# A block-fused transformer kernel: VectorE keeps the first half of each weight residue, GpSimd takes the second

## The reference

```python
# block 2 (second_block)
hid = silu(x @ w_gate) * (x @ w_up)
ffn = hid @ w_down
ple = sigmoid(x @ w_ple_gate) * (p @ w_ple)
x = layer_norm(ALPHA * x + ffn + ple, ln2_g, ln2_b)
# block 3 (conv_ffn)
u = h @ w_up
uc = conv_b + sum(shift(u, 2 - i) * conv_w[i] for i in range(3))
gate, val = split(uc, 2)
y = (silu(gate) * val) @ w_down
```

## Time and profile before

| what | value |
|---|---|
| median of 3 runs | 4415.32 us (4413.2 to 4418.15) |
| profiled execution | 4419.46 us, its span 4418.1 us |
| PE busy | 3849.8 us (87%) |
| VectorE busy | 2018.2 us (46%) |
| ScalarE busy | 1107.3 us (25%) |
| GpSimd busy | 80.8 us (2%) |
| mean granted TensorE clock | 0.917 of full |

### The profile page before, as it was taken

The page is one execution under the profiler, slowest core; times in us unless marked ns, Lnnn a source line. Parts: engine busy times, 40 slices in busy tenths (PEclk is TensorE's granted clock), DMA queues, the critical chain, the costliest instruction groups (busy, mean ns, idle before and its releaser), DMA issues. The chain is left out here.

```text
span 4418.1 us, 59550 instructions
## 1 busy us (share of the span) xinstructions
PE 3849.8 (87%) x24448; PEld 3504.7 (79%) x24448; DVE 2018.2 (46%) x2880; ACT 1107.3 (25%) x1261; POOL 80.8 (2%) x151
## 2 busy tenths in 40 slices
PE   6997889999998979446999999995998769999897
PEld 5885678888887867235999999994875669999897
DVE  1554134344445445553555544444121246766545
ACT  1001122222220000001444433332011034444333
POOL 0000010000000001000000000000000000000000
PEclk9998988888888989768999999997998889999998
DMA  4675211111115748213455554451332234444453
GB/s 192 262 300 185 86 44 52 59 50 40 40 40 206 307 181 339 95 48 105 154 190 189 189 179 177 178 182 69 143 129 90 86 114 171 180 162 179 161 192 143
DMA packets 90682, 650.42 MB, mean 147 GB/s; under 512 B 10065, under 2 KB 10577, under 8 KB 12370
## 3 DMA queue, kind: packets, MB, share of 16 engines
q1 hardware_dynamic: 74304, 540.05, 33.8%
q0 software_dynamic: 13824, 100.67, 5.7%
q10 hardware_dynamic: 2450, 8.16, 0.5%
HBM read 646.74 MB, written 2.10 MB: 147 GB/s over the span
## 5 line engine op out<-in xcount | busy, mean ns | idle before, releaser
L391 PE MATMUL ps<-work,ring 128*128 128x256 f32 x5920 | 1298.2, 382 | 40.4 <-DVE work L1576 10.9
L391 PEld LDWEIGHTS ps<-work,ring 128*128 128x128 f32 x5920 | 1132.0, 192 | 200.6 <-DVE work L1576 11.8
L1338 DVE TENSOR_TENSOR ring_parts<-ring,ring_hi 128x1024 fp32r<-128x1024 f32 x568 | 689.3, 1225 | 726.2 <-ACT ring_hi L920 725.7
L920 ACT ACTIVATE ring_hi<-ring 128x1024 fp32r<-128x1024 f32 x568 | 599.3, 1059 | 940.0 <-PE ps L416 939.9
L414 PE MATMUL ps<-x_hi,ring_hi 128*128 128x256 f32 x1664 | 465.6, 280 | 22.4 <-DVE x_lo L1674 22.4
L415 PE MATMUL ps<-x_lo,ring_hi 128*128 128x256 f32 x1664 | 462.2, 278 | 0.0
L416 PE MATMUL ps<-x_hi,ring_parts 128*128 128x256 f32 x1664 | 460.4, 277 | 0.0
L414 PE MATMUL ps<-h_hi,ring_hi 128*128 128x256 f32 x1408 | 399.6, 284 | 48.0 <-DVE ring_parts L1338 26.2
L414 PE MATMUL ps<-hid_hi,ring_hi 128*128 128x256 f32 x1392 | 394.3, 283 | 37.3 <-DVE gu L1700 19.3
L415 PE MATMUL ps<-h_lo,ring_hi 128*128 128x256 f32 x1408 | 395.5, 281 | 0.0
L416 PE MATMUL ps<-h_hi,ring_parts 128*128 128x256 f32 x1408 | 394.7, 280 | 0.0
(11 more groups left out here) (371 smaller groups left out, 3935.6 us busy)
## 6 DMA issues: line engine op xcount, KB each, us to landing
ring<-in_weights SPq DMA_DIRECT2D x511, 1024.0 KB, 4.8
work<-in_ada POOLq DMA_DIRECT2D x96, 1024.0 KB, 8.1
resid<-in_lora ACTq DMA_DIRECT2D x9, 256.0 KB, 2.6
resid<-in_x SPq DMA_DIRECT2D x1, 2048.0 KB, 13.4
resid<-in_x ACTq DMA_DIRECT2D x1, 2048.0 KB, 8.8
out<-work SPq DMA_DIRECT2D x4, 512.0 KB, 2.6
con<-in_const ACTq DMA_DIRECT2D x1, 1666.0 KB, 13.6
con<-in_const ACTq DMA_DIRECT2D x1, 1028.0 KB
```

What stands on the lines that cost most here:

```text
L391: ins = mm(PS[:, b + m // 2, (m % 2) * T:(m % 2 + 1) * T], ws[:, k, m * P:(m + 1) * P], rhs(kc), start=(kc == 0 and m % 2 == 0), stop=(kc ...
L920: A(HI[:, 2 * (e % 2) + half, :], ring[:, n % RING, half * (SLOT // 2):(half + 1) * (SLOT // 2)], ACT.Copy)\
L1338: tt(lo, x, HI[:, e % 4, :].bitcast(F32), ALU.subtract).then_inc(S("lo_ready"), 1)
```

## The change

A slot's two residues get an engine each. VectorE subtracts the first half of each slot and counts in `lo_even`. GpSimd subtracts the second half and counts in `lo_odd`, in two loops of four slots a trip: 38 trips over `ffn2` and `down2`, which stand behind `fetch_modulations(1)`, and 33 trips over `ffn3` and `down3`, which stand behind the zeroing of `UP3`. TensorE waits for `lo_even` before a first half and for `lo_odd` before a second. Operands, shapes and ScalarE's part are as they were.

```diff
@@ by_parts (TensorE)
                 for half in range(2):
-                    v = 2 * e + half + 1
-                    pe.wait_ge(S("lo_ready"), v if i is None else v + i * 2 * step)
+                    pe.wait_ge(S("lo_even" if half == 0 else "lo_odd"), e + 1 if i is None else e + 1 + i * step)
@@ GpSimd
         fetch_modulations(1)
+        def split_odd(first, slots):
+
+            with gp.Fori(0, slots // RING) as i:
+                for n in range(first, first + RING):
+                    e = 2 * SPLIT_AT[n] + 1
+                    gp.wait_ge(S("hi_ready"), i * (2 * RING) + (e + 1))
+                    x, lo = (r[:, n % RING, SLOT // 2:SLOT] for r in (ring, ring_parts))
+                    gp.tensor_tensor(lo, x, HI[:, e % 4, :].bitcast(F32), ALU.subtract).then_inc(S("lo_odd"), 1)
+
+        split_odd(slot0("ffn2"), slot0("misc") - slot0("ffn2"))
         gp.wait_ge(S("ds_stored"), 2)
         gp.wait_ge(S("x3_ready"), 1)
         gp.memset(UP3.rearrange("p a b -> p (a b)"), 0.0).then_inc(S("up_zeroed"), 1)
+        split_odd(slot0("ffn3"), SLOTS - slot0("ffn3"))
@@ VectorE
         def split(first, count, i=None, step_=0):
 
             for n in range(first, first + count):
-                for half in range(2):
-                    e = 2 * SPLIT_AT[n] + half
-                    v.wait_ge(S("hi_ready"), e + 1 if i is None else e + 1 + i * 2 * step_)
-                    x, lo = (r[:, n % RING, half * (SLOT // 2):(half + 1) * (SLOT // 2)] for r in (ring, ring_parts))
-                    tt(lo, x, HI[:, e % 4, :].bitcast(F32), ALU.subtract).then_inc(S("lo_ready"), 1)
+                e = 2 * SPLIT_AT[n]
+                v.wait_ge(S("hi_ready"), e + 1 if i is None else e + 1 + i * 2 * step_)
+                x, lo = (r[:, n % RING, 0:SLOT // 2] for r in (ring, ring_parts))
+                tt(lo, x, HI[:, e % 4, :].bitcast(F32), ALU.subtract).then_inc(S("lo_even"), 1)
```

## The result

The changed kernel takes 4494.91 us (median of 4 runs, 4492.51 to 4497.81) against 4414.26 of the kernel before (4 runs): the ratio on record is 1.0175, 95% interval 1.0162 to 1.0188. By the medians it is 80.6 us slower. (The ratios given here are those on record; they differ from the quotients of the two medians by up to 0.0012.) The forecast was slower as well, but by 45 us, and the time lies 5 us above the stated range.

A forecast was written before the change was run, and what follows sets the result against it. TensorE, busy 87% of the span, was taken to bound the kernel, with its waits for VectorE's chains deciding. The terms +35 + 8.4 + 2.8 - 1.0 - 0.9 - 0.2 = +44 us gave 4460 us, range 4403 to 4490.

The forecast's parts named there:

- ten waits of ffn3: Trip ends in ffn3: GpSimd holds VectorE's chain, so TensorE's residue comes 3.5 us later, ten times: +35 us, bounds 0 and 10 x 5.1.
- short waits in mid-trip: Middle of each ffn3 trip: the prediction gave no term for TensorE waits there, so 0.
- rest of ffn3, clock above all: Behind the ffn3 waits: the clock falls after the other four too, 4 x 2.1 = +8.4 us, bounds 0 and +21.
- two starts: Starts of ffn2 and ffn3: GpSimd's first residues delay line 1724 and the input's residue, +2.8 us, bounds 0 and +6.
- block 2, between start and end: End of ffn2 and down2: gains shrink under GpSimd's holds, leaving -1.0 and -0.9 us.
- end of ffn3: End of ffn3: TensorE is stopped and no residue comes free, so the gain keeps -0.2 us.
- matmul pace of down3: Matmuls of down3: the prediction gave no term for a slower pace, so 0.
- GpSimd's duration: GpSimd's subtraction of one half: 1.9 us from its copies' rows, bounds 1.04 and 2.7 us.
- The removal: Residues leaving VectorE: waits shorten by 2.1 us in ffn3, 2.1 at ffn2's end, 4.4 in down2, together -8.6 us.
- the engines don't hold each other: Rival on VectorE and GpSimd: neither holds the other, only the -8.6 us remain, 4407 us; chance 0.25.
- GpSimd yields: Rival on the ffn3 chain: GpSimd enters only at the pause after `hid_lo`, +1.4 us ten times, 4433 us; chance 0.2.
- GpSimd is the bound: Rival on all 284 slots: the subtraction exceeds 5.55 us, TensorE waits each slot; at 6 us +128, 4543 us; chance 0.03.

The follow-up runs named there:

- runs with zeros: Changed kernel, loops written out with constant waits, GpSimd filling its half with zeros instead of subtracting: 4404.78 us, 0.9979 of the kernel before.
- with a copy: Changed kernel, loops written out with constant waits, GpSimd copying its half onto itself instead of subtracting: 4430.86 us, ratio 1.0042 to the kernel before.
- ffn3 back on VectorE: Changed kernel, but VectorE subtracts both halves in ffn3 and GpSimd keeps second halves of ffn2, down2 and most of down3: 4413.61 us, ratio 0.9996.
- the early residue: Kernel before, all on VectorE, subtracting TensorE's next slot between lines 1875 and 1877 of each ffn3 trip but the last: 4377.52 us, ratio 0.9908.
- the halves swapped: Changed kernel, but GpSimd takes the first half of each slot and VectorE the second: 4462.88 us, ratio 1.0112 to the kernel before.
- The control: Changed kernel with only GpSimd's two loops written out and constant waits in place of register values: 4492.64 us, ratio 1.0171 to the kernel before.

## Why the prediction was wrong, step by step

The direction, the mechanism and the stage were right: GpSimd's operation holds VectorE on the chain of ffn3, shown by the runs with zeros and with a copy, with ffn3 back on VectorE, and with the early residue. The size was not. By the terms of the sum, in the profile's time (predicted +44, measured +76; each pause of TensorE is counted from start to start of the matmuls around it, less the usual distance):

| term | predicted | measured |
|---|---|---|
| ten waits of ffn3 | +35 | +50.4 |
| short waits in mid-trip | 0 | +9.3 |
| rest of ffn3, clock above all | +8.4 | +9.2 |
| two starts | +2.8 | +3.0 |
| block 2, between start and end | -1.9 | -1.2 |
| end of ffn3 | -0.2 | +1.0 |
| matmul pace of down3 | 0 | +4.4 |

- **The step that failed** is in the bullet on the ten waits: "beside line 1864, which has one SBUF input; I take 0 (upper bound 1)". That line (1873 after) was held for 1.1 us at the end of each trip, so there are three holds on the chain and not two. No row of before showed a one-input operation of VectorE beside GpSimd, and I took the good end. The delay then carried on: it moved the second hold from the gap behind line 1884 onto the eight operations of line 1879, and the third onto the cast. The run with the copy shows the other case. There the first operation of the chain is not held, and the next hold lies behind line 1884 of the change, where I had put it.
- **GpSimd's duration** was the second part: 1.9 us taken from the copies, 2.41 measured (2.46 in the mean). It lay within the bounds. The estimate of 2.25 from the Trainium skill, "GPSIMD Engine Reference", section "Performance versus the Vector engine", is nearer; the measurement decides. Together the two errors make 5.0 us a trip and not 3.5, and 15 of the 32 us missed.
- **The range.** The ten waits alone stayed within their bound (+50.4 of +51), though by three shorter holds and not by two of 2.7 us. What carried the time past 4490 are terms that stood in no bound: the short waits, and the matmul pace of down3.
- **The short waits** are the second term that I had at nothing, without a reason. I worked out the end of a trip and not its middle. Before, the first residue behind the gate group ended at 3788.3 and TensorE came to its half at 3790.8, so 2.5 us were free; the holds on lines 1873 and 1879 are 1.05 and 2.25 us, 3.3 in sum. The hold on line 1873 is what makes the difference: with the halves swapped it is absent there (1.38 us) while line 1879 is still held (5.66), and no short wait is left.
- **Clock.** Taken as 8.4, measured 9.2 as the rest of ffn3, and the agreement is in part luck. As forecast, the clock falls behind all ten waits and not behind six. But the price of 2.1 us for a fall came from a stretch that was slow for another reason too: its matmuls ran 0.1178 us apart and not 0.1155. A stretch of the kernel before with the same fall and the usual pace, 384 matmuls, takes 46.0 and not 46.5 us:

```profile
3912.40:3958.40 46.00, 45.96 (x384) 45.96 (x384) 30.30 (x43) 21.25 (x20) 0.00 (x0) 0.96 0.48 177
```

  So a fall costs about 1.6 us. After the change there are four more, and some last longer: up to 6.2 us of half clock while TensorE runs, where no stretch of ffn3 had more than 3.5 before.
- **The removal** was right, but for a slip (three times 1.4 is 4.2 and not 4.4): -8.6 worked out, -9.3 measured with GpSimd only writing, and -7.6 in the three kinds of waits of its trace. Its part in block 2 was mostly lost to holds in the change, as said.
- **The end of ffn3** went the other way, by 1.0: line 1873 is held there too, the same miss.
- **Down3.** 190 us of it at clock 1.00 hold 1647 matmuls before and 1615 after:

```profile
4260.00:4450.00 190.00, 190.00 (x1615) 190.00 (x1614) 44.80 (x42) 73.15 (x69) 82.83 (x35) 1.00 0.54 190
```

It isn't GpSimd's doing. The control has GpSimd at work and 1646, and the early residue alone has 1615 with GpSimd at rest. Nor is it down3's: the profiled execution of the run with zeros has 1616 in 190 us of ffn2, where the kernel before has 1647, and three stretches of ffn3 between two waits had this pace before the change. So the +4.4 can't be put down to the change. What sets this pace stays open.

Of the rivals, "the engines don't hold each other" and "GpSimd yields" fell by the durations above: with the copy line 1885 was held, and after the change GpSimd began at 3831.60 amid the eight operations of line 1879 and was not made to wait (2.44 us). "GpSimd is the bound" fell as well: with 2.46 us in a slot of 5.55 no wait names it.

## What to carry to other kernels

A share of work given to GpSimd costs what it does to VectorE's other instructions, and that is read from the chains that another engine waits for, not from busy time. Count every VectorE instruction on such a chain whose inputs all lie in SBUF, the one-input ones too, as held until GpSimd's operation ends, if that one reads, and do so for each place in a trip that has little free time, not for its end alone. And look first at the order on the chain: moving the two residues of one slot forward in each trip brought 43 us with no second engine, where the second engine could have brought 9 at best.

## What was not expected of the hardware

- VectorE's one-input operation with per-partition scalars (line 1873, 128x256 in float32, 410 ns alone) is held by a GpSimd operation that reads: four take 2.50 us and not 1.38. The Trainium skill, "SBUF — State Buffer", section "Who interferes with whom", counts copies, casts and `tensor_scalar` among the operations that can contend with GpSimd; the trace agrees, and I had read past that list.
- Operations of VectorE with one input from PSUM and one from SBUF are not held. In down2 of the changed kernel GpSimd's subtraction spans the whole of line 1707 and most of line 1709, and they take 1.21 and 1.22 us, as they do alone; the cast in ffn2, with both ends in SBUF, takes 2635 ns (694 alone).

```profile
2697.97 1.21 DVE L1707 TENSOR_TENSOR work<-ps,work 128x1024 f32<-128x1024 f32 x1
2699.22 1.22 DVE L1709 TENSOR_TENSOR gu<-ps,work 128x1024 f32<-128x1024 f32 x1
...
2696.92 3.33 POOL L1307 TENSOR_TENSOR ring_parts<-ring,ring_hi 128x1024 fp32r<-128x1024 f32 x1
```

- A GpSimd operation that only writes leaves VectorE's two-input operations alone (the residues beside it stay at 1224 ns) and still holds a cast (1151 ns against 694).
- The hold is mutual: who comes second waits, GpSimd too (2.93 us against 2.41, and 1.49 against 1.04).
- A wait of 1 us more per trip can cost more than itself. With the copy the ten waits grew by 9.6 us and the whole stage by 22; the rest is the clock, 0.95 of full in the stage against 0.98.
